# Forgetting attention: head pairs by key tile, values of two heads in 64 columns each, sums from added probabilities

## What is computed

```python
def forgetting_attention(q, k, v, logf):
    ...
    F = jnp.cumsum(jnp.pad(logf.transpose(0, 2, 1), ((0, 0), (0, 0), (0, pad))), axis=-1)
    ...
        s = jnp.einsum('bhqd,bhkd->bhqk', qi, kh, preferred_element_type=jnp.float32) * scale
        s = s + Fi[..., None] - F[:, :, None, :]
        s = jnp.where(kpos[None, :] <= pi[:, None], s, -jnp.inf)
        p = jax.nn.softmax(s, axis=-1)
        return jnp.einsum('bhqk,bhkd->bhqd', p.astype(vh.dtype), vh)
```

## Time and profile before

| what | us |
|---|---|
| median of 3 runs | 1911.0 |
| lowest and highest run | 1910.67, 1911.49 |
| the profiled execution | 1911.65 |
| its span | 1909.9 |
| TensorE busy in the span | 1891.4 |
| VectorE, ScalarE, GpSimd busy | 1390.7, 961.2, 120.4 |

### The profile page before, as it was taken

The page is one execution under the profiler, slowest core; times in us unless marked ns, Lnnn a source line. Parts: engine busy times, 40 slices in busy tenths (PEclk is TensorE's granted clock), DMA queues, the critical chain, the costliest instruction groups (busy, mean ns, idle before and its releaser), DMA issues.

```text
span 1909.9 us, 26755 instructions
## 1 busy us (share of the span) xinstructions
PE 1891.4 (99%) x9040; PEld 1522.3 (80%) x9040; DVE 1390.7 (73%) x2201; ACT 961.2 (50%) x1356; POOL 120.4 (6%) x163
## 2 busy tenths in 40 slices
PE   9999999999999999999999999999999999999998
PEld 9987888877777788876678888888886788888887
DVE  7986444575999866788857888853397778888533
ACT  5667433456777633678754333333366543333332
POOL 0200000001000000045600000000101000000000
PEclk9999999999999999999999999999999999999999
DMA  5220333326999625510013333333341133333332
GB/s 196 84 73 11 92 97 99 99 83 217 359 358 349 221 64 162 136 50 3 3 46 100 97 91 97 99 100 110 99 127 35 56 99 96 92 98 99 99 111 88
DMA packets 68634, 219.39 MB, mean 115 GB/s; under 512 B 11648, under 2 KB 14880, under 8 KB 68416
## 3 DMA queue, kind: packets, MB, share of 16 engines
q1 hardware_dynamic: 64240, 212.46, 34.3%
q10 hardware_dynamic: 4304, 5.77, 1.2%
HBM read 209.05 MB, written 2.10 MB: 111 GB/s over the span
## 4 chain that ended last, share of the span: by engine, by line
PE 91%; DVE 5%; ACT 2%; DMA 1%; issue 1%; SPq 0%; DVEq 0%; ACTq 0%
PE psum L1212 63%; PE psum L1735 7%; PE psum L1709 2%; PE psum L1937 2%; PE psum L1754 2%; PE psum L1646 1%; PE psum L1718 1%; PE psum L1384 1%; PE psum L2124 1%; PE psum L1902 1%; PE psum L1910 1%; PE psum L1789 1%; PE psum L1855 1%; DVE sig L3492 1%; DVE psum L4305 1%
## 5 line engine op out<-in xcount | busy, mean ns | idle before, releaser
L1212 PE MATMUL psum<-x_hi,w_hi 128*128 128x512 f32 (+1 forms) x1336 | 490.6, 378 | 0.0
L1212 PE MATMUL psum<-x_hi,w_lo 128*128 128x512 f32 (+1 forms) x1336 | 486.9, 375 | 0.0
L1212 PE MATMUL psum<-x_lo,w_hi 128*128 128x512 f32 (+1 forms) x1336 | 486.8, 375 | 0.0
L3183 DVE TENSOR_TENSOR w_lo<-raw,w_hi 128x1024 fp32r<-128x1024 f32 x243 | 296.2, 1220 | 184.1 <-ACT w_hi L2246 183.7
L2246 ACT ACTIVATE w_hi<-raw 128x1024 fp32r<-128x1024 f32 x243 | 256.0, 1055 | 185.1 <-DMA raw<-stream 184.5
L1212 PEld LDWEIGHTS psum<-x_hi,w_hi 128*128 128x128 f32 x1336 | 245.0, 188 | 46.9 <-issue 1.7
L1212 PEld LDWEIGHTS psum<-x_lo,w_hi 128*128 128x128 f32 x1336 | 245.0, 188 | 45.7 <-issue 1.2
L1212 PEld LDWEIGHTS psum<-x_hi,w_lo 128*128 128x128 f32 x1336 | 244.9, 188 | 45.4
L1212 PE MATMUL psum<-hid_hi,w_hi 128*128 128x512 f32 (+3 forms) x710 | 261.4, 376 | 0.5 <-DVE hid_lo L4420 0.5
L1212 PE MATMUL psum<-hid_hi,w_lo 128*128 128x512 f32 (+3 forms) x710 | 260.1, 374 | 0.0
L1212 PE MATMUL psum<-hid_lo,w_hi 128*128 128x512 f32 (+3 forms) x710 | 260.0, 374 | 0.0
(11 more groups left out here) (706 smaller groups left out, 2940.3 us busy)
## 6 DMA issues: line engine op xcount, KB each, us to landing
raw<-stream SPq DMA_DIRECT2D x251, 512.0 KB, 3.6
raw<-experts SPq DMA_DIRECT2D x70, 512.0 KB, 5.2
raw_more<-experts SPq DMA_DIRECT2D x68, 512.0 KB, 5.3
staged<-staged ACTq DMA_DIRECT2D x64, 64.0 KB, 3.2
resid<-x_fm SPq DMA_DIRECT2D x3, 528.0 KB, 7.6
consts<-consts_in SPq DMA_DIRECT2D x1, 1373.0 KB, 14.2
staged<-staged SPq DMA_DIRECT2D x20, 64.0 KB, 2.4
out_fm<-resid SPq DMA_DIRECT2D x4, 320.0 KB, 2.3
```

Source lines behind the costliest of these rows:

```text
L1212: last = pe.matmul(o, wt[:, slot, k * P:(k + 1) * P], m[part], start=start and p == 0, stop=stop and p == 2, skip_group_check=True)
L3183: dve.tensor_tensor(w_lo[:, slot, :], raw[:, slot, :], w_hi[:, slot, :].bitcast(F32), ALU.subtract)\
```

## The change

- `F_STEPS` goes by key tile, both heads of a tile one after the other: 512, 512, 400, 400, 272, 272, 144, 144, 16, 16 columns.
- The value products of a tile are issued together for the two heads, each with 64 columns of weights (values alone), into the two halves of one bank (`fox_values`). Tile (i - 3) / 2 stands behind steps 3, 5, 7 and 9; tile 4 stands behind step 1 of the next pair (in the last pair behind `conv_square_sum`).
- GpSimd adds the probabilities of tiles 1, 2 and 3 onto those of tile 0, six adds a pair (`add_fox_probs`), the first once tile 0's values are multiplied. TensorE multiplies the sum, and the probabilities of tile 4, with 64 columns of ones for each head into the halves of a second bank (`fox_sums`), behind the values of tile 4.
- ScalarE copies the two banks whole (`keep_fox_values`, `keep_fox_sums`) behind steps 1 and 2 of the next pair. Waits of the exponentials follow the new tiles of probabilities.
- Tiles are placed anew; the copy of the first pair no longer waits for the convolution. The counts of `probs_added` in the second attention start 24 higher. In the last pair VectorE runs `conv_centred` ahead of a low part of the outputs.

```diff
-F_STEPS = [(_half, _j) for _half in range(2) for _j in range(F_TILES)]
+F_STEPS = [(_half, _j) for _j in range(F_TILES) for _half in range(2)]
...
+N_FADDS = 2 * (F_TILES - 2)
+N_FOUT = F_TILES + 1
+FOX_ADDED = N_FADDS * FOX_PAIRS
...
-        def fox_probs(n, j):
-            return EV[:, n % 3, 2:2 + SEQ - fox_first(j)]
+        def fox_values_bank():
+            return PS[:, 4, :]
+
+        def fox_sums_bank():
+            return PS[:, 6, :]
+
+        def fox_probs(p, half, j):
+            width = SEQ - fox_first(j)
+            if j == 0:
+                return FIRSTF[p % 2][:, half, :]
+            if j == 1:
+                return EV[:, half, 2:2 + width]
+            start = sum(SEQ - fox_first(x) for x in range(2, j))
+            return LASTF[:, start:start + width] if half else EV[:, 2, 2 + start:2 + start + width]
...
+            def add_fox_probs(p, j):
+
+                whole = fox_first(j)
+                for half in range(2):
+                    k = 2 * (j - 1) + half
+                    pool.wait_ge(fexp_done, N_F * p + 2 * j + half + 1)
+                    if k == 0:
+
+                        pool.wait_ge(fpv_done, N_FOUT * p + 1)
+                    if k >= 2:
+
+                        pool.wait_ge(probs_added, N_FADDS * p + k - 1)
+                    first = FIRSTF[p % 2][:, half, whole:SEQ]
+                    pool.tensor_tensor(first, first, fox_probs(p, half, j), ALU.add).then_inc(probs_added, 1)
...
+            def fox_values(p, j):
+
+                pe.wait_ge(fexp_done, N_F * p + 2 * j + 2)
...
+                for half in range(2):
+                    mm = pe.matmul(fox_values_bank()[half * HD:(half + 1) * HD, fox_first(j):SEQ], V1[:, j, p, 2 * half * HD:(2 * half + 1) * HD],
+                                   fox_probs(p, half, j), start=j == 0, stop=j == QT, skip_group_check=True)
+                mm.then_inc(fpv_done, 1)
+
+            def fox_sums(p):
+
+                pe.wait_ge(probs_added, N_FADDS * (p + 1))
...
+                for j in (0, QT):
+                    for half in range(2):
+                        mm = pe.matmul(fox_sums_bank()[half * HD:(half + 1) * HD, fox_first(j):SEQ], V1[:, j, p, HD:2 * HD],
+                                       fox_probs(p, half, j), start=j == 0, stop=j == QT, skip_group_check=True)
+                mm.then_inc(fpv_done, 1)
...
-                    if i >= 2:
-                        fox_outputs(p, i - 2)
-                    elif p:
-                        fox_outputs(p - 1, N_F + i - 2)
-            for i in range(N_F - 2, N_F):
-                fox_outputs(FOX_PAIRS - 1, i)
+                    if i == 1 and p:
+                        fox_values(p - 1, QT)
+                        fox_sums(p - 1)
+                    if i >= 3 and i % 2:
+                        fox_values(p, (i - 3) // 2)
             conv_square_sum()
+            fox_values(FOX_PAIRS - 1, QT)
+            fox_sums(FOX_PAIRS - 1)
...
+                if i == 0 and p > 1:
+
+                    act.wait_ge(fpv_done, N_FOUT * (p - 1))
...
+                if i in (2, 4) and p:
+
+                    act.wait_ge(fpv_done, N_FOUT * (p - 1) + (2 if i == 2 else F_TILES))
+                    act.wait_ge(probs_added, N_FADDS * (p - 1) + (2 if i == 2 else N_FADDS))
+                act.activation(fox_probs(p, half, j), fox_score_bank(n)[:, 0:SEQ - fox_first(j)], ACT.Exp).then_inc(fexp_done, 1)
...
+            def keep_fox_values(p):
+
+                act.wait_ge(fpv_done, N_FOUT * p + F_TILES)
+                act.activation(OWF[p][:, :], fox_values_bank(), ACT.Copy).then_inc(fo_kept, 1)
+
+            def keep_fox_sums(p):
+
+                act.wait_ge(fpv_done, N_FOUT * (p + 1))
+                act.activation(SUMF[p][:, :], fox_sums_bank(), ACT.Copy).then_inc(fo_kept, 1)
...
                     if i == 1 and p:
-                        keep_fox(p - 1, 1)
-                    if i == F_TILES + 1:
-                        keep_fox(p, 0)
+                        keep_fox_values(p - 1)
+                    if i == 2 and p:
+                        keep_fox_sums(p - 1)
```

More of the change, by code:

```diff
@@ L390, in build @@
         QMF0 = over("fox_q_and_rows_even", [P, 2, SEQ], F32R)
-        OWF = [over(f"fox_o_{p}", [P, SEQ], at=ow_at if p == 0 else ks_at + (FOX_PAIRS + p - 1) * pair_bytes) for p in range(FOX_PAIRS)]
+        OWF = [over(f"fox_o_{p}", [P, SEQ], at=ks_at + (FOX_PAIRS + p) * pair_bytes) for p in range(FOX_PAIRS)]
         cursor[0] = ks_at
@@ L418, in build @@
         AFTERF = placed("fox_causal_mask", ts_at + T1 * 4, [P, SEQ])
-        SUMF = [placed(f"fox_sums_{p}", ts_at + 2 * T1 * 4 if p == 0 else arena_at + ks_at + (p - 1) * pair_bytes, [P, SEQ]) for p in range(FOX_PAIRS)]
+        SUMF = [placed(f"fox_sums_{p}", arena_at + ks_at + p * pair_bytes, [P, SEQ]) for p in range(FOX_PAIRS)]
+        FIRSTF = [placed("fox_probs_summed_even", more_at, [P, 2, SEQ]), placed("fox_probs_summed_odd", w_hi_at + (U["merge"] + 3) % SLOTS * UNIT * 4, [P, 2, SEQ])]
+        LASTF = placed("fox_probs_last", ts_at + 2 * T1 * 4, [P, SEQ])
         LOW32 = placed("conv_out", arena_at + 2 * FC * SEQ * 4 - C * T1 * 4, [P, C * T1])
@@ L1088, in _ @@
                 .then_inc(forms_set, 1)
+            def add_fox_probs(p, j):
[9 more added lines that the diff above has]
+                    pool.tensor_tensor(first, first, fox_probs(p, half, j), ALU.add).then_inc(probs_added, 1)
+            for p in range(FOX_PAIRS):
+                for j in range(1, QT):
+                    add_fox_probs(p, j)
             pool.wait_ge(act_asked, 4)
@@ L1135, in add_third @@
                     tail = PSUMMED[row][:, SEQ // 2:SEQ]
-                    pool.wait_ge(probs_added, N_ADDS * p + END_ADDED[6 + row])
+                    pool.wait_ge(probs_added, FOX_ADDED + N_ADDS * p + END_ADDED[6 + row])
                     pool.tensor_tensor(tail, tail, probs_of(p, i)[:, SEQ // 2 * half:SEQ // 2 * (half + 1)], ALU.add).then_inc(probs_added, 1)
@@ L1367, in fox_scores @@
                 pe.matmul(s, KSF2[:, half, p, k0:k0 + P], QMF[p % 2][:, half, q0:SEQ], start=False, stop=True, skip_group_check=True).then_inc(fs_done, 1)
[L1369 to L1374, removed]
+            def fox_values(p, j):
+                pe.wait_ge(fexp_done, N_F * p + 2 * j + 2)
                 if j == 0 and p == 0:
-                    pe.wait_ge(lin_free, R["q1b"] + half)
-                if j == QT and n < N_F:
+                    pe.wait_ge(lin_free, R["q1b"])
+                if j == 0 and p:
+                    pe.wait_ge(fo_kept, 2 * p - 1)
+                if j == QT and p == 0:
                     pe.wait_ge(forms_set, 8)
[L1381 to L1385, removed]
+                for half in range(2):
[4 more added lines that the diff above has]
+                pe.wait_ge(probs_added, N_FADDS * (p + 1))
+                if p == 0:
+                    pe.wait_ge(lin_free, R["q1b"] + 1)
+                else:
+                    pe.wait_ge(fo_kept, 2 * p)
+                for j in (0, QT):
[3 more added lines that the diff above has]
+                mm.then_inc(fpv_done, 1)
             def residual(name, t, src, ready):
@@ L1951, in whole_sums @@
             def whole_sums(p):
-                pe.wait_ge(probs_added, N_ADDS * (p + 1))
+                pe.wait_ge(probs_added, FOX_ADDED + N_ADDS * (p + 1))
                 for row in range(4):
@@ L2545, in fox_exps @@
             def fox_exps(p, i):
-                j, n = F_STEPS[i][1], N_F * p + i
+                half, j = F_STEPS[i]
+                n = N_F * p + i
                 act.wait_ge(fs_done, n + 1)
-                if n == 0:
+                if i == 0 and p > 1:
+                    act.wait_ge(fpv_done, N_FOUT * (p - 1))
+                if i == 2 and p == 0:
                     act.wait_ge(fq_ready, 6)
[L2553 to L2566, removed]
+                if i in (2, 4) and p:
[8 more added lines that the diff above has]
+                act.activation(SUMF[p][:, :], fox_sums_bank(), ACT.Copy).then_inc(fo_kept, 1)
             def fox_output_high(p):
@@ L2596, in _ @@
             root_table()
-            keep_fox(FOX_PAIRS - 1, 1)
+            keep_fox_values(FOX_PAIRS - 1)
+            keep_fox_sums(FOX_PAIRS - 1)
             act.wait_ge(sq_used, S0["ln"] + SUMS["ln"])
@@ L2889, in exps @@
                     if j >= 2 and q + 1 < PAIRS2:
-                        act.wait_ge(probs_added, N_ADDS * q + ADDED_BY[j])
+                        act.wait_ge(probs_added, FOX_ADDED + N_ADDS * q + ADDED_BY[j])
                 if i < 2:
@@ L3603, in _ @@
                     fox_queries_low(3)
+                if p == FOX_PAIRS - 1:
+                    conv_centred()
                 if p > 1:
                     fox_output_low(p - 2)
-                if p == FOX_PAIRS - 1:
-                    conv_centred()
                 if p:
```

4 lines of the change are left out of this document (1 added, 3 removed).

## The result

| | before | after |
|---|---|---|
| median, 22 executions each | 1911.54 | 1914.59 |
| lowest, highest | 1910.67, 1914.06 | 1912.67, 1917.76 |
| ratio to before, 95% interval | | 1.0013 [1.0008, 1.0019] |
| profiled execution, its span | 1911.65, 1909.9 | 1913.71, 1912.0 |
| the four pairs, sum | 13.01, 13.06, 13.05, 13.44: 52.56 | 12.49, 13.51, 13.52, 14.53: 54.05 |

The account below looks back on a forecast made before the run. TensorE, busy 99% of the span, was taken as the bound. Products -0.1, pair-end waits +1.5, last pair +0.5 and first pair -0.2 summed to +1.7: profiled 1913.35, median 1912.7 us, range 1909.2 to 1916.2.

Parts of the forecast that it names:

- The total: Whole kernel: +1.7 us, profiled 1913.35, median 1912.7, slower by 0.09%, counted as the same.
- the waits: TensorE's waits in the stage: +1.5 at pair ends, +0.5 in the last pair, -0.2 in the first; range +0.7 to +2.7.
- the products: Value and sum products on TensorE over four pairs: 19.9 us against 20.0 before, so -0.1; range -1.5 to +3.3.
- After the stage: What follows the four pairs: nothing lost, 3.8 us of cover for VectorE's last low part; merge starts 1.5 to 2 us later.
- The switch: Entry and exit of each of twenty side-by-side groups: mean 0.32 us a group, 6.4 in all; ends 0.27 and 0.45.
- The dear switch: Rival at the twenty groups' entries and exits: short neighbours make it 0.5 a group, 3.6 us more, 1916.3 us; chance 0.17.
- the free one: Rival at the twenty groups: changing tile shape costs nothing, 6.4 us come off, 1907.3 us; chance 0.06.
- Small passes: Two side-by-side products of 16 columns a pair, four passes at 0.08 us each: 0.32 a pair.
- The waits at the end: TensorE's wait before the next pair's first score grows from 0.43 to some 0.93: +1.5 over three transitions, ends +0.9 and +2.1.
- The first and the last pair: First pair: third score waits less, -0.2. Last pair: ScalarE presses, sixth score waits some 0.5, +0.5, ends 0 and 0.8.
- The cover: Time between GpSimd's additions ending and the sums needing them: 3.4 us in three pairs, some 1.8 in the last.
- Costing GpSimd at nothing: GpSimd's additions, 5.4 us a pair, are hidden by the time before the sums and add nothing.

Follow-up runs that it names:

- early turn: Changed kernel with the four transposes of the maxima one step earlier and both row copies behind step 7: 1911.75 us, ratio to before 0.9999.
- sums in the wait: Changed kernel with the first three pairs' sums and tile 4 values at the pair's own end, in one group with tile 3's values: 1910.02 us.
- two groups: Kernel with the sums in the wait, values of tiles 1 to 3 all behind step 9, two groups a pair instead of four: 1912.83 us.
- additions late: As two groups, but tile 0's values behind step 5 with tile 1's, so GpSimd's additions start later: 1915.66 us, ratio to before 1.0024.
- three and two groups: Kernel with the sums in the wait, tile 1's values moved behind step 7 (three) or tiles 1 to 3 behind step 9 (two): 1911.89 and 1912.83 us.

## Why the prediction was right

- **The total.** The profiled execution was put at 1913.35 and took 1913.71; the stage was put at +1.7 and came at +1.5. Two small misses lie in that: the waits were put at +1.8 (1.5 + 0.5 - 0.2), recorded idle time rose by 2.0, and the products were put at -0.1, busy time fell by 0.5. The median was put at 1912.7 and is 1914.6, inside the range; its +3.0 isn't the sum's doing alone (last point). The kernel is steadily, if barely, slower: the interval leaves out 1, which the forecast's 0.09% foretold in sign.
- **After the stage.** Nothing was put there. Merge starts 1.6 later than before (second product, 184.22 against 182.62), as the +1.5 to 2 of the text said, and the span ends 2.1 later. The difference stays 1.6 up to 810 us; then TensorE waits for VectorE in the second attention, in both profiled executions of the changed kernel (0.37 in the other), where it didn't before:

```profile
815.26 0.47 PE L1905 MATMUL psum<-keys_hi_twice,q_parts_first_even 128*128 128x512 f32 x1 [0.40 <-DVE maxima L4151]
```

The difference is 2.2 there, goes back to 1.7 as a wait of 0.37 for VectorE at 1384 us falls away, and is 2.0 by 1518 us. Why VectorE comes later there is open.
- **The switch**, mean 0.32 a group: measured 0.37, 0.29, 0.32 and 0.37; the group of tile 3 ends in the wait and can't be read. The exit and the entry do shrink beside short neighbours, as put. The dear switch (0.5) is refuted, the free one too.
- **Small passes** were the mis-sized term of the products: 0.32 a pair was put, 0.17 measured. At 0.03 to 0.08 apart they don't pay the 0.11 of a full weight load. With that the products are 4 x (2.21 + 0.85 + 0.17) + 4 x (0.37 + 0.29 + 0.32 + 0.37 + 0.27) = 19.4, where the last 0.27 is still the prediction's: -0.6 for the -0.1, and busy time says -0.5.
- **The waits at the end**, 0.43 to 0.93 on three transitions: turn to next pair 3.31 for 3.3 to 3.4. By the profile's idle time they grew from 0.23 to 0.89, 2.0 in three, since part of the 0.43 before is recorded as busy; TensorE's recorded work in the stretch is 2.42 for the 2.38 put. The early turn and the sums in the wait show that this is where the gain went: fill the wait, and 3.8 us of stage come back.
- **The first and the last pair.** In the first, the third score waits 0.25 by its start instead of 0.35, so -0.1 for the -0.2. The last was put at 14.9 and took 14.53. ScalarE did press: the sums' copy at 175.11, a high part at 175.72, and two exponentials from 176.26; but the sixth score waited some 0.3 in place of 0.5. The times that the prediction lists for it give 2.25 less 2.01, 0.24; the other half of its 0.5 it doesn't derive.
- **GpSimd**: the additions took 5.4 us in the last pair, as put, and ended 12.05 us into it (12.3 put). The cover was 1.08 and not 1.8 because the sums came sooner than put, 13.1 us into the pair for 14.1 (additions end at 181.74, sums start at 182.82). In the second pair it was 3.75; the 3.4 of the text should be 3.6 by its own 15.9 and 12.3. Costing GpSimd at nothing was nearly right, 0.13 to 0.17 a pair; what it does to VectorE had been left out (below).
- **What the prediction had no step for** is the clock: 1.00 in each window before, and so taken as given. The two profiled executions after the change have a full clock up to their last 5 us, and they are 2.1 and 2.2 above the one before; the medians are 3.0 apart. The other 0.9 may come with executions of lower clock, which the changed kernel has more often as far as the means tell; no trace of it shows one.

## What to carry to other kernels

Before columns are taken from an engine that is busy 99% of the time, find the waits in which it spends the last per cent, and ask on which side of them the saved work lies. Here half the columns fell away ahead of a hand-over that was timed by another engine, and only moving other work into that wait turned a loss of 3 us into a gain of 1.7 (not clear of nothing), and 2.8 (clear of it) with one change of shape a pair fewer and the rows copied sooner. Count the changes of tile shape (0.3 to 0.4 us each here), and merge groups only on the side of the hand-over where nobody waits for their place. And look at what work given to an idle engine does to the steps of its neighbours: a step of 0.16 that becomes 0.66 costs little until it ends a wait.

## What the runs showed of the hardware that I had not expected

**The granted clock falls in the middle of a nearly full stage.** Of the twelve profiled executions (that of the kernel before among them) eight kept 1.00 through the whole stage; four (both without the additions, two groups, additions late) had one stretch of about 3.5 us at 0.50, the level of 1.2 GHz, and lost 1.5 to 1.7 us each. Ahead of it TensorE had, in turn, score products of 16 columns and a wait of 0.89; scores of 144 and 16 columns with short waits on ScalarE; a wait of 1.80. The Trainium skill (TensorE: Matmul & The Clock Gate, Part 1) says that the clock is set by how busy the engine has been of late, and that the number of slow matmuls in one kernel varies from run to run. The rows agree with the second, as the kernel without the additions had its fall in the last pair once and in the second pair the other time; for the first they show only what stood ahead of each fall, and that the same waits could pass without one.

**VectorE and GpSimd hold each other up.** The last of VectorE's steps before the turn combines two columns. Beside the additions it takes four times as long. Before the change, and after it, at the third pair's end:

```profile
165.31 0.17 DVE L3560 TENSOR_TENSOR fox_maxima<-fox_maxima,meta_maxima 128x2 f32<-128x2 f32 x1
```

```profile
165.67 0.65 DVE L3614 TENSOR_TENSOR fox_maxima<-fox_maxima,meta_maxima 128x2 f32<-128x2 f32 x1
```

In the last pair it goes both ways: VectorE's two sums of the convolution took 2.15 (1.29 before), GpSimd's 272 columns 1.21 where 0.76 is usual. The runs without the additions settle the cause. In both executions the step is back at its old length in every pair, and the two sums take 1.29 again (here the second execution, third pair):

```profile
166.62 0.16 DVE L3609 TENSOR_TENSOR fox_maxima<-fox_maxima,meta_maxima 128x2 f32<-128x2 f32 x1
```

With them the step starts 0.1 us into GpSimd's second addition of 272 columns and ends 0.02 after it, in each of the first three pairs (the addition ends at 139.27, 152.78 and 166.30, the step at 139.29, 152.79 and 166.32) and in six other profiled executions alike. The Trainium skill (SBUF — State Buffer, Who interferes with whom) says that a VectorE instruction with two inputs in SBUF and a GpSimd instruction that reads it contend for a pair of ports, which one of them holds alone; these ends agree with it. As the turn follows that very step, this is where "free" additions on GpSimd touch the critical path: of the 0.13 that the second and third pair gained without them, 0.09 lie ahead of the turn (10.19 us into the second pair, 10.10 without them), and in the kernels with three and two groups the same lengthening is, by the estimate above, some 0.5 of each wait of 0.50 to 0.79.
